# Hybrid attention trunk on one core: probability blocks turned four at a time, keys stored last 16 first, norms, splits and rotary rows in another order

## The chip, the core and the metric

The kernel is one program on one NeuronCore of a Trainium2 chip. The metric is the device time of one execution in microseconds (us), as a median of runs. TensorE is called PE, VectorE DVE, ScalarE ACT, GpSimd POOL; SP only issues DMAs.

## The reference

The reference runs four layers over T = 272 tokens (16 meta tokens, 256 of the sequence) with D = 1024. Each layer is a token mixer with 16 heads, then a gated MLP with a causal width-3 convolution; each half ends in `layer_norm(alpha*h + out)`. The mixers are, in order: FoX (forgetting attention), SWA (sliding window 128, two key/value heads, rotary, sinks), MLA (latent attention: nope part 64 wide, rotary part 32 wide, one rotary key shared by all heads), and FoX again.

```
s = q @ k.T * scale (+ decay[t] - decay[s])      # causal; SWA also within 128, meta keys always seen
p = softmax(s);  o = p @ v;  mix = o @ w_o
h = layer_norm(alpha*h + mix);  u = conv3(h @ w_in);  ffn = (silu(u_g) * u_v) @ w_out
h = layer_norm(alpha*h + ffn)
```

## The kernel before

Activations lie transposed: channels on partitions, all 272 tokens on the free axis. Every dense product is three fp32r matmuls of 128 x 128 weights by 272 columns (high weight by high input L385, high by low L388, low by high L389). A *unit* is 128 x 1024 fp32 weights (512 KB) in a ring of four slots: SP loads it (L344), ACT rounds it to `w_hi` (L839, `split_hi`), DVE subtracts to `w_lo` (L1260 inside `split_lo`). ACT and DVE each run a written order; a split for a unit three ahead stands at a fixed place in every turn of a loop, and DVE's split waits for ACT's of the same unit (`hi_ready`). All engines run their instructions strictly in that order and meet by semaphores.

Attention goes head by head, in pairs of heads, m = 0..7, overlapped with the projections of the next pair. The queries of a head stand in three chunks (`CHUNKS`: 16, 128, 128 queries, seeing 16, 144, 272 keys), side by side in 432 columns. For one head:

- PE: scores (L518 for FoX and SWA, L499 for MLA; FoX first adds the decay, L512), into a PSUM bank.
- DVE `mask_scores` (L1320): mask and row minimum. ACT `exps` (L886, L889): exponentials and row sums into `probs`. DVE `normalise` (L1335, L1338).
- PE `turn` (L535): six transposes of `probs`. ACT `copy_turned` (L901, L902): PSUM to `probs_t`.
- PE `mix` (L553): values by probabilities, three key blocks (272, 144 and 16 query columns) for two heads. ACT `out_hi` (L908) and DVE `out_lo` split the result for the output projection.

In SWA, DVE's turn m is: `out_lo(m-4)`, mask of heads 2m-4 and 2m-3, `rope_q(m-1)`, normalise of both heads, the split of a unit, and the evacuation of the query panel (L1565), for which PE's swap matmul (L690) waits. ACT's turn m is: `out_hi(m-4)`, exps of head 2m-4, two `copy_turned`, exps of head 2m-3, the `w_hi` of a unit. PE's: scores of pair m-2, turns of heads 2m-6 and 2m-5, swap, panel, mix of pair m-3; the last two turns stream the output projection (L404) in place of panels.

In MLA the reciprocal root of the key latent is made for all columns (ones matmuls L730, ACT root, DVE reciprocal L1640); the rotary key rows are copied to all 16 heads by POOL (L1217, L1222), the rotary query rows to `queries` by four 32-row DVE adds (`rope_r`); `take_k` (DVE, two ops) empties the key panel and stands between the two normalises; the next scores wait for it.

At the start of the MLP's second half (`output`, n odd) ACT loads its function table (L933) and then splits the first weights of `down`.

## Time and profile before

| | us |
|---|---|
| median of 3 runs (lowest, highest) | 1333.57 (1332.96, 1334.44) |
| profiled execution, its own time | 1333.88 |
| its span | 1332.1 |
| PE matmul busy | 1296.4 (97%) |
| DVE / ACT / POOL busy | 938.3 / 793.8 / 225.8 |

The span runs from the first instruction to the last; the execution's own time has 1.8 us more around it. PE is called busy from a matmul's start to its modelled end, which lies well after the next can start, so stalls are read from the distance of starts. The layers' attention stretches lie at about 47 to 130 us (FoX), 362 to 435 (SWA), 676 to 765 (MLA) and 1027 to 1110 (FoX).

### The profile page before, as it was taken

What the parts mean: (1) busy time and instruction counts of PE and PEld (TensorE: products, weight loads), DVE (VectorE), ACT (ScalarE), POOL (GpSimd) and SP (SyncE); (2) the same over time, 40 slices, a digit from 0 to 9 for tenths busy, and PEclk for the clock granted to TensorE, in tenths of its full rate; (3) what the DMA queues carried; (4) which work ended last, traced back from release to release, by engine and by line L of the source; (5) the groups of instructions that cost most, each with busy time, mean ns of one, the idle gap of its engine ahead of it and who ended that gap; (6) DMA issues with size and microseconds to landing.
All of it is one profiled execution on the core that took longest, in us unless ns stands there. A gap on an engine that the chain in (4) does not pass through costs nothing.

```text
span 1332.1 us, 29945 instructions
## 1 busy us (share of the span) xinstructions
PE 1296.4 (97%) x10381; PEld 1252.5 (94%) x10381; DVE 938.3 (70%) x1877; ACT 793.8 (60%) x1625; POOL 225.8 (17%) x208
## 2 busy tenths in 40 slices
PE   7999999999998999999998999999999999999997
PEld 7999999999887999999987899999999899999997
DVE  4765877765787877765678687776567667777665
ACT  4565666654565676664476667666446565766643
POOL 1000044420000034330001003433000000244300
PEclk9999999999999999999998999999999999999999
DMA  7432465556421455556442045555645334465562
GB/s 267 140 110 80 143 189 185 178 180 198 133 91 49 130 185 184 180 155 213 155 127 80 33 143 187 187 172 165 208 139 158 111 112 127 144 187 189 174 218 83
DMA packets 56723, 202.80 MB, mean 152 GB/s; under 512 B 6208, under 2 KB 8256, under 8 KB 56512
## 3 DMA queue, kind: packets, MB, share of 16 engines
q1 hardware_dynamic: 56640, 201.68, 47.4%
q8 instruction: 54, 0.88, 0.3%
q14 instruction: 29, 0.24, 0.1%
HBM read 200.61 MB, written 1.05 MB: 151 GB/s over the span
## 4 chain that ended last, share of the span: by engine, by line
PE 82%; DVE 7%; ACT 5%; issue 3%; DMA 1%; POOL 1%; ACTq 0%; DVEq 0%; POOLq 0%; SPq 0%
PE ps L385 23%; PE ps L389 22%; PE ps L388 22%; PE ps L535 2%; PE ps L553 2%; ACT probs L889 2%; DVE w_lo L1260 1%; PE ps L424 1%; PE ps L518 1%; PE ps L430 1%; PE ps L427 1%; ACT w_hi L839 1%; DMA raw<-in_weights 1%; POOL gated L1234 1%; DVE scores L1320 1%
## 5 line engine op out<-in xcount | busy, mean ns | idle before, releaser
L1260 DVE TENSOR_TENSOR w_lo<-raw,w_hi 128x1024 fp32r<-128x1024 f32 x377 | 461.1, 1225 | 230.3 <-ACT w_hi L839 228.9
L385 PE MATMUL ps<-h_hi,w_hi 128*128 128x272 f32 (+1 forms) x1752 | 508.6, 290 | 1.8 <-DVE q_rope L1526 1.0
L389 PE MATMUL ps<-h_hi,w_lo 128*128 128x272 f32 (+1 forms) x1752 | 505.8, 289 | 0.0
L388 PE MATMUL ps<-h_lo,w_hi 128*128 128x272 f32 (+1 forms) x1752 | 499.6, 285 | 0.0
L839 ACT ACTIVATE w_hi<-raw 128x1024 fp32r<-128x1024 f32 x377 | 395.0, 1050 | 147.7 <-PE ps L385 136.9
L385 PEld LDWEIGHTS ps<-h_hi,w_hi 128*128 128x128 f32 x1752 | 329.1, 188 | 8.4 <-issue 5.4
L388 PEld LDWEIGHTS ps<-h_lo,w_hi 128*128 128x128 f32 x1752 | 330.0, 188 | 0.3
L389 PEld LDWEIGHTS ps<-h_hi,w_lo 128*128 128x128 f32 x1752 | 328.9, 188 | 0.0
L385 PE MATMUL ps<-hid_hi,w_hi 128*128 128x272 f32 (+2 forms) x636 | 185.4, 292 | 2.2 <-DVE w_lo L1260 1.9
L388 PE MATMUL ps<-hid_lo,w_hi 128*128 128x272 f32 (+2 forms) x636 | 183.1, 288 | 0.0
L389 PE MATMUL ps<-hid_hi,w_lo 128*128 128x272 f32 (+2 forms) x636 | 183.0, 288 | 0.0
L1234 POOL TENSOR_TENSOR gated<-y 128x272 f32<-128x272 f32 x88 | 134.6, 1530 | 274.8 <-DVE y L1681 260.6
L1181 ACT ACTIVATE y<-ps,cst 128x272 f32<-128x272 f32 x176 | 100.0, 568 | 63.5 <-PE ps L389 61.8
L1208 POOL TENSOR_TENSOR h<-h,y 128x272 f32<-128x272 f32 x16 | 12.0, 774 | 707.1 <-ACT y L938 707.1
L385 PEld LDWEIGHTS ps<-hid_hi,w_hi 128*128 128x128 f32 x636 | 121.3, 191 | 3.7 <-issue 2.8
L388 PEld LDWEIGHTS ps<-hid_lo,w_hi 128*128 128x128 f32 x636 | 121.4, 191 | 0.4
L389 PEld LDWEIGHTS ps<-hid_hi,w_lo 128*128 128x128 f32 x636 | 121.2, 191 | 0.0
L1679 DVE SCALAR_TENSOR_TENSOR y<-ps,cst,y 128x271 f32<-128x271 f32 x176 | 87.4, 497 | 29.8 <-ACT y L1181 26.8
L1681 DVE SCALAR_TENSOR_TENSOR y<-ps,cst,y 128x270 f32<-128x270 f32 x176 | 87.8, 499 | 26.8 <-DVE y L1679 26.8
L889 ACT ACTIVATE probs<-scores,stats 16x16 f32<-16x16 f32 (+2 forms) x192 | 76.9, 401 | 46.0 <-DVE stats L1320 46.0
L388 PE MATMUL ps<-hid,w_hi 128*128 128x272 f32 (+1 forms) x288 | 82.1, 285 | 0.0
L389 PE MATMUL ps<-hid,w_lo 128*128 128x272 f32 (+1 forms) x288 | 82.0, 285 | 0.0
(184 smaller groups left out, 1727.3 us busy)
## 6 DMA issues: line engine op xcount, KB each, us to landing
raw<-in_weights SPq DMA_DIRECT2D x377, 512.0 KB, 3.7
cst<-in_consts SPq DMA_DIRECT2D x1, 1795.5 KB, 12.1
h<-in_x SPq DMA_DIRECT2D x2, 544.0 KB, 5.8
out<-h SPq DMA_DIRECT2D x8, 128.0 KB, 1.7
```

What stands on the lines that cost most here:

```text
L385: m = pe.matmul(b, whi, xhi, start=n == 0, stop=False)
L388: pe.matmul(b, whi, xlo, start=False, stop=False)
L389: m = pe.matmul(b, wlo, xhi, start=False, stop=n == len(tiles) - 1)
L535: return pe.transpose(b[0:keys_n, col:col + q], pr[0:q, c0:c0 + keys_n], ident[0:q, 0:q])
L553: ins = pe.matmul(ps[HD * s:HD * s + HD, 6, lo:T], v_tok[:, t, col:col + HD], probs_t[:, s, c0:c0 + T - lo], start=n == 0, stop=n == 2)
L839: act.activation(w_hi[slot][:], raw[slot][:], ACT.Copy).then_inc(hi_ready, 1)
L889: ins = act.activation(probs[0:r, hn % 4, PCOL[ch]:PCOL[ch] + hi], scores[0:r, s, SCOL[ch]:SCOL[ch + 1]], ACT.Exp, scale=-1.0, bias=stats[ ...
L1181: act.activation(y[:, j, :], bank(pu + j), ACT.Identity, scale=col(2), bias=col(3)).then_inc(conv_begun, 1)
L1234: pool.tensor_tensor(gated[:], y[:, 2 * slot, :], y[:, 2 * slot + 1, :], ALU.mult).then_inc(gate_mul, 1)
L1260: return dve.tensor_tensor(out_, a_, b_, op)
L1679: own.link(dve.scalar_tensor_tensor(yj[:, 1:T], b[:, 0:T - 1], col(1), yj[:, 1:T], ALU.mult, ALU.add))
L1681: dve.scalar_tensor_tensor(yj[:, 2:T], b[:, 0:T - 2], col(0), yj[:, 2:T], ALU.mult, ALU.add).then_inc(bank_free, 1)
```

## The change

Scores are laid out in another order: chunk 1 first (144 columns), chunk 0 (16), chunk 2 (272), and in chunk 2 and in `keys` the last 16 keys stand before the other 256. So the three narrow probability blocks (keys 128 to 143 of chunk 1, chunk 0, keys 256 to 271 of chunk 2) are 48 neighbouring columns, and `turn` is four transposes of 128 columns instead of six. `copy_turned` takes three instructions for two. The third matmul of `mix` has 48 columns, written in three groups of 16; its values (keys 128 to 143, 0 to 15, 256 to 271) are put under each other by two small DMAs issued by ACT (`corner_values`). Evacuations of keys become two instructions each (16 and 256 columns).

Beside this: in FoX `take_k` stands between the two splits; in SWA the first split follows the evacuation of keys and values, and DVE's turn has a new order; in MLA the key scale is spread by PE from the token-wise one (`lat_spread`), POOL's copies and DVE's 32-row adds become DMAs issued by ACT (one of 32 x 16 x 272 elements, and four of 32 x 272 for each of the four `place_rope`), and `take_k` stands straight after the masks; the table load of `down` comes one panel later.

```diff
-SCOL = (0, 16, 160, 432)
-SW = SCOL[3]
-
-PCOL = (0, P, 3 * P)
-PW = PCOL[2] + T
-
-
 TAIL = T - 2 * P
-PT1, PT2, PTW = T, T + P + TAIL, T + P + 2 * TAIL
+
+
+SCOL = ((P + TAIL, P + 2 * TAIL), (0, P + TAIL), (P + 2 * TAIL, P + 2 * TAIL + T))
+SW = SCOL[2][1]
+KCOL = ((TAIL, 2 * TAIL), (TAIL, P + 2 * TAIL), (0, T))
+
+
+TURNED = (0, P + 3 * TAIL, 2 * P + 3 * TAIL, P)
+PT1, PT2, PTW = T, T + P, T + P + 3 * TAIL
...
                 for ch, (lo, hi) in enumerate(CHUNKS):
-                    m = pe.matmul(ps[0:hi - lo, 2 + s, SCOL[ch]:SCOL[ch + 1]], q[:, lo:hi], key[:, 0:hi],
+                    m = pe.matmul(ps[0:hi - lo, 2 + s, slice(*SCOL[ch])], q[:, lo:hi], key[:, slice(*KCOL[ch])],
                                   start=True, stop=True)
                 m.then_inc(scored, 1)
...
-                def one(col, ch, key, keys_n=P):
-
-                    q = P
-                    c0 = PCOL[ch] + key
-                    return pe.transpose(b[0:keys_n, col:col + q], pr[0:q, c0:c0 + keys_n], ident[0:q, 0:q])
-
-
-                one(PT1 + TAIL - P, 1, P)
-                one(PTW - P, 2, 2 * P, TAIL)
-                one(0, 0, 0)
-                one(N_META, 1, 0)
-                one(N_META + P, 2, 0)
-                one(PT1 + TAIL, 2, P).then_inc(transposed, 1)
+                for n, col in enumerate(TURNED):
+                    t = pe.transpose(b[:, n * P:(n + 1) * P], pr[:, col:col + P], ident)
+                t.then_inc(transposed, 1)
 
             def mix(a, kind, m):
 
                 pe.wait_ge(pt_copied, HEADS * a + 2 * m + 2)
                 pe.wait_ge(o_split, PAIRS * a + m)
-                for n, (t, lo, c0) in enumerate(((0, 0, 0), (1, P, PT1), (2, 2 * P, PT2))):
+                if m == 0:
+                    pe.wait_ge(v_corners, 32 * (a + 1))
+                for t in range(3):
                     for s in range(2):
                         hn = 2 * m + s
                         col = (hn // 8 if kind == "swa" else hn) * HD
-                        ins = pe.matmul(ps[HD * s:HD * s + HD, 6, lo:T], v_tok[:, t, col:col + HD],
-                                        probs_t[:, s, c0:c0 + T - lo], start=n == 0, stop=n == 2)
+                        o, pt = ps[HD * s:HD * s + HD, 6], probs_t[:, s]
+                        if t < 2:
+                            dst, src = o[:, (0, N_META + P)[t]:T], pt[:, (0, PT1)[t]:(PT1, PT2)[t]]
+                        else:
+                            dst = o[:, 0:3 * P].rearrange("p (g c) -> p g c", g=3)[:, :, 0:TAIL]
+                            src = pt[:, PT2:PTW].rearrange("p (g c) -> p g c", g=3)
+                        ins = pe.matmul(dst, v_tok[:, t, col:col + HD], src, start=t == 0, stop=t == 2)
                 ins.then_inc(mixed, 1)
 
...
                         is_q = ks[0] == 0
                         for k in ks:
                             pe.wait_ge(lat_sq, k + 1)
-                            if not is_q:
-                                pe.matmul(ps[:, 6, 0:T], ones, y[:, k % 4, :], start=k == ks[0], stop=k == ks[-1])
...
                     swap(gated[:])
+                    pe.wait_ge(lat_scale, 1)
+                    for n, (lo, hi) in enumerate(((0, P), (P, 2 * P), (2 * P, T))):
+                        ins = pe.matmul(ps[:, 6, lo:hi], lat_col[0:hi - lo, 1, n:n + 1].broadcast_to([hi - lo, P]),
+                                        ident[0:hi - lo, 0:hi - lo], start=True, stop=True)
+                    ins.then_inc(lat_spread, 1)
                     for n in range(6):
...
+                            pe.wait_ge(rope_key, 16)
                         if m:
-                            pe.wait_ge(rope_key, (m - 1) // 2 + 1)
-                        if m:
-                            pe.wait_ge(roped, base + 2 + (m - 1) // 2)
+                            pe.wait_ge(rope_rows[(m - 1) // 2], 64)
                             pe.wait_ge(q_taken, m)
...
+            def corner_values(cols):
+
+                for n, chunk in enumerate((1, 0)):
+                    act.dma_start(v_tok[TAIL * n:TAIL * n + TAIL, 2, 0:cols],
+                                  v_tok[0:TAIL, chunk, 0:cols]).then_inc(v_corners, 16)
...
-                act.activation(probs_t[:, s, 0:PT2], ps[:, 4 + s, 0:PT2], ACT.Copy)
-                act.activation(probs_t[0:TAIL, s, PT2:PTW], ps[0:TAIL, 4 + s, PT2:PTW],
+                b = ps[:, 4 + s]
+                act.activation(probs_t[:, s, N_META:PT2], b[:, 0:3 * P], ACT.Copy)
+                act.activation(probs_t[0:32, s, PT2:PT2 + 2 * TAIL].rearrange("p (g c) -> p g c", g=2),
+                               b[0:32, 3 * P:4 * P].rearrange("p (g c) -> p g c", c=TAIL)[:, 0:8:7, :], ACT.Copy)
+                act.activation(probs_t[32:48, s, PT2 + 2 * TAIL:PTW], b[32:48, 4 * P - TAIL:4 * P],
                                ACT.Copy).then_inc(pt_copied, 1)
...
                     k = i * 4 + j
+                    if k == 1 and n % 2:
+                        act.preload_act_table_set(TABLES)
                     if k:
                         square(n, k - 1)
 
-                if n % 2:
-                    act.preload_act_table_set(TABLES)
...
                     latent_root(lat_col[:, 0, :], ps[:, 5, 0:3], 0).then_inc(lat_std, 1)
-                    latent_root(squares[:, 1, :], ps[:, 6, 0:T], 1).then_inc(lat_std, 1)
                     act.preload_act_table_set(TABLES)
...
+                    def place_rope(r):
+
+                        act.wait_ge(roped, ROPED0 + r + 1)
+                        for t in range(4):
+                            act.dma_start(queries[64:96, 4 * r + t, :],
+                                          totals[32 * t:32 * t + 32, r % 2, :]).then_inc(rope_rows[r], 16)
+
                     for r in range(2):
                         take_r(r)
+                    act.wait_ge(lat_spread, 1)
+                    act.activation(squares[:, 1, :], ps[:, 6, 0:T], ACT.Copy).then_inc(lat_std, 1)
                     split_unit(ur + AHEAD)
                     for n in range(6):
                         copy_vt(n)
                         if n == 0:
+                            act.wait_ge(key_roped, 1)
+                            act.dma_start(keys[64:96, :, :], rope_parts[:, 2 * T:3 * T].unsqueeze(1).broadcast_to(
+                                [32, HEADS, T])).then_inc(rope_key, 16)
                             split_unit(uv + AHEAD)
+                        if n == 2:
+                            place_rope(0)
                     split_unit(uv + 1 + AHEAD)
                     for r in range(2):
                         split_panel(a, "qk", r)
                         take_r(2 + r)
+                    place_rope(1)
+                    act.wait_ge(vt_copied, 6)
+                    corner_values(D)
                     for m in range(PAIRS + 1):
+                        if m in (3, 6):
+                            place_rope(m // 3 + 1)
                         if m >= 4:
...
-                    pool.wait_ge(key_roped, 1)
-                    pool.tensor_copy(keys[64:96, 0:4, :],
-                                     scores[0:32, 0, 0:T].unsqueeze(1).broadcast_to([32, 4, T])).then_inc(rope_key, 1)
-                    pool.wait_ge(rope_key, 1)
-                    pool.wait_ge(masked, HEADS * a + 2)
-                    for j in range(1, 4):
-                        pool.tensor_copy(keys[64:96, 4 * j:4 * j + 4, :],
-                                         keys[64:96, 0, :].unsqueeze(1).broadcast_to([32, 4, T])).then_inc(rope_key, 1)
-                    pool.wait_ge(rope_key, 4)
...
-                        copy(keys[:, m, :], b).then_inc(bank_free, 2)
+                        copy(keys[:, m, 0:TAIL], b[:, 2 * P:T])
+                        copy(keys[:, m, TAIL:T], b[:, 0:2 * P]).then_inc(bank_free, 2)
...
                         if m < PAIRS:
                             split_units(a, "qk", 0, 2 * m)
-                            if m == 0:
-                                take_k(m)
+                            take_k(m)
                             split_units(a, "qk", 0, 2 * m + 1)
-                            if m:
-                                take_k(m)
...
-                    split_units(a, "vk", 0, 0)
                     for j in range(2):
                         dve.wait_ge(panel_done, pv + j + 1)
                         vk_evac(0, j, bank(pv + j), pv + j)
+                    split_units(a, "vk", 0, 0)
...
-                                ins = copy(keys[64 * r:64 * r + 64, g, :], q_rope[64 * g:64 * g + 64, 0, :])
+                                src = q_rope[64 * g:64 * g + 64, 0, :]
+                                copy(keys[64 * r:64 * r + 64, g, 0:TAIL], src[:, 2 * P:T])
+                                ins = copy(keys[64 * r:64 * r + 64, g, TAIL:T], src[:, 0:2 * P])
...
-                    for m in range(PAIRS + 2):
-                        if m >= 4:
-                            out_lo(a, m - 4)
-                        if m >= 2:
+                    for m in range(PAIRS + 3):
+                        if m >= 3:
+                            normalise(a, kind, 2 * m - 5)
+                        if 2 <= m < PAIRS + 2:
                             mask_scores(a, kind, 2 * m - 4)
                             mask_scores(a, kind, 2 * m - 3)
                         if 1 <= m <= PAIRS:
                             rope_q(m - 1)
-                        if m >= 2:
-                            normalise(a, kind, 2 * m - 4)
-                            normalise(a, kind, 2 * m - 3)
+                        if 4 <= m < PAIRS + 2:
+                            out_lo(a, m - 4)
                         if m < PAIRS:
                             split_units(a, "q", 0, m)
+                        if 2 <= m < PAIRS + 2:
+                            normalise(a, kind, 2 * m - 4)
+                        if m < PAIRS:
                             dve.wait_ge(panel_done, pq + m + 1)
...
-                        for t in range(4):
-                            r = slice(32 * t, 32 * t + 32)
-                            ins = tt(queries[64:96, 4 * m + t, :], y[r, 0, :], y[r, 1, :], ALU.add)
-                        ins.then_inc(roped, 1)
+                        if m >= 2:
+                            dve.wait_ge(rope_rows[m - 2], 64)
...
-                        tt(keys[0:64, 2 * m, :], b[0:64], kv_rstd[0:64], ALU.mult)
-                        tt(keys[0:64, 2 * m + 1, :], b[64:128], kv_rstd[64:128], ALU.mult).then_inc(bank_free, 2)
+                        for s in range(2):
+                            r = slice(HD * s, HD * s + HD)
+                            tt(keys[0:64, 2 * m + s, 0:TAIL], b[r, 2 * P:T], kv_rstd[r, 2 * P:T], ALU.mult)
+                            ins = tt(keys[0:64, 2 * m + s, TAIL:T], b[r, 0:2 * P], kv_rstd[r, 0:2 * P], ALU.mult)
+                        ins.then_inc(bank_free, 2)
...
                     dve.wait_ge(lat_std, 2)
-                    own.link(dve.reciprocal(kv_rstd, kv_rstd))
...
+                        if m < PAIRS:
+                            take_k(m)
                         if 4 <= m < PAIRS:
                             out_lo(a, m - 4)
                         if m:
                             normalise(a, kind, 2 * m - 2)
-                        if m < PAIRS:
-                            take_k(m)
-                        if m:
                             normalise(a, kind, 2 * m - 1)
                         if m < PAIRS:
                             split_units(a, "qk", 0, 2 + 2 * m)
```

Two places show the new order. The first is DVE in a middle turn of SWA, between `rope_q` and the masks of the next turn. `hid_lo` is `out_lo`, `rinv` and `probs` are `normalise`, `w_lo` is the split, `queries<-ps` the evacuation. Before:

```order
L1335 RECIPROCAL rinv<-rinv 128x3 [waits dve_own]
L1338 TENSOR_SCALAR probs<-probs,rinv 16x16 [waits dve_own]
L1338 TENSOR_SCALAR probs<-probs,rinv 128x144
L1338 TENSOR_SCALAR probs<-probs,rinv 128x272
L1260 TENSOR_TENSOR rinv<-stats,sink_exp 128x3 [waits exped]
L1335 RECIPROCAL rinv<-rinv 128x3 [waits dve_own]
L1338 TENSOR_SCALAR probs<-probs,rinv 16x16 [waits dve_own]
L1338 TENSOR_SCALAR probs<-probs,rinv 128x144
L1338 TENSOR_SCALAR probs<-probs,rinv 128x272
L1260 TENSOR_TENSOR w_lo<-raw,w_hi 128x1024 [waits hi_ready]
L1565 TENSOR_SCALAR queries<-ps 128x272 [waits panel_done]
L1260 TENSOR_TENSOR hid_lo<-ps,hid_hi 128x272 [waits o_hi,bank_free]
```

And in the change:

```order
L1287 TENSOR_TENSOR queries<-y 128x272 [waits dve_own]
L1287 TENSOR_TENSOR hid_lo<-ps,hid_hi 128x272 [waits o_hi]
L1287 TENSOR_TENSOR w_lo<-raw,w_hi 128x1024 [waits hi_ready]
L1287 TENSOR_TENSOR rinv<-stats,sink_exp 128x3 [waits exped]
L1362 RECIPROCAL rinv<-rinv 128x3 [waits dve_own]
L1365 TENSOR_SCALAR probs<-probs,rinv 16x16 [waits dve_own]
L1365 TENSOR_SCALAR probs<-probs,rinv 128x144
L1365 TENSOR_SCALAR probs<-probs,rinv 128x272
L1596 TENSOR_SCALAR queries<-ps 128x272 [waits panel_done]
L1287 TENSOR_TENSOR rinv<-stats,sink_exp 128x3 [waits exped,bank_free]
L1362 RECIPROCAL rinv<-rinv 128x3 [waits dve_own]
L1365 TENSOR_SCALAR probs<-probs,rinv 16x16 [waits dve_own]
```

Both normalises stood ahead of the split; now both stand behind it, one on each side of the evacuation, and the masks of the next turn follow the second.

The second is ACT in MLA at the start of turn m = 6 (`place_rope(3)`), in the change:

```order
L914 ACTIVATE probs_t<-ps 16x16
L1134 DMA queries<-totals 32x272 [waits roped]
L1134 DMA queries<-totals 32x272 x3
L920 ACTIVATE hid_hi<-ps 128x272 [waits mixed]
L898 ACTIVATE probs,stats<-scores,stats 16x16 [waits transposed,masked]
```

Four DMAs now stand in ACT's queue ahead of `out_hi` and of the exponentials.

## Rows read from the trace of the kernel before

**Rows 1.** The page: the chain that ended last, by engine
```profile
PE 82%; DVE 7%; ACT 5%; issue 3%; DMA 1%; POOL 1%; ACTq 0%; DVEq 0%; POOLq 0%; SPq 0%
```

**Rows 2.** Groups of PE by shape: columns as on the page; transposes, ones matmuls
```profile
L535 PE MATMUL ps<-cst,probs 128*128 128x128 f32 x320 | 47.8, 274 | 0.0
...
L730 PE MATMUL ps<-y,cst 128*128 128x272 f32 x4 | 1.1, 392 | 0.0
```

**Rows 3.** Timeline of PE in FoX: start, us, instruction [idle before, releaser]
```profile
56.02 0.47 PE L512 MATMUL ps<-dec,pick 64*128 64x432 f32 x2 [0.99 <-issue]
...
60.47 1.47 PE L535 MATMUL ps<-cst,probs 128*128 128x128 f32 x12
```

**Rows 4.** Timeline of DVE in FoX, the second key evacuation
```profile
55.48 0.43 DVE L1499 COPY keys<-ps 128x272 f32<-128x272 f32 x1
```

**Rows 5.** Timeline of DVE in SWA, one turn
```profile
401.85 0.21 DVE L1320 CUSTOM_DVE_ANT_0 scores<-ps,cst,neg_sinks 16x16 f32<-16x16 f32 x1
...
406.63 0.17 DVE L1260 TENSOR_TENSOR rinv<-stats,sink_exp 128x3 f32<-128x3 f32 x1 [0.80 <-ACT probs L889]
...
407.66 1.20 DVE L1260 TENSOR_TENSOR w_lo<-raw,w_hi 128x1024 fp32r<-128x1024 f32 x1
408.80 0.42 DVE L1565 TENSOR_SCALAR queries<-ps 128x272 f32<-128x272 f32 x1
409.25 0.44 DVE L1260 TENSOR_TENSOR hid_lo<-ps,hid_hi 128x272 fp32r<-128x272 f32 x1
409.61 0.21 DVE L1320 CUSTOM_DVE_ANT_0 scores<-ps,cst,neg_sinks 16x16 f32<-16x16 f32 x1
```

**Rows 6.** Timeline of ACT in SWA, the same turn
```profile
402.81 0.30 ACT L886 ACTIVATE sink_exp<-stats,cst 128x3 f32<-128x3 f32 x1 [2.75 <-DVE stats L1320]
...
404.21 0.49 ACT L901 ACTIVATE probs_t<-ps 128x416 f32<-128x416 f32 x1
...
405.13 0.28 ACT L886 ACTIVATE sink_exp<-stats,cst 128x3 f32<-128x3 f32 x1
...
406.51 1.04 ACT L839 ACTIVATE w_hi<-raw 128x1024 fp32r<-128x1024 f32 x1
```

**Rows 7.** Timeline of PE at the start and the end of SWA
```profile
362.83 0.40 PE L385 MATMUL ps<-h_hi,w_hi 128*128 128x272 f32 x1 [0.99 <-DVE q_rope L1526]
...
427.38 1.00 PE L553 MATMUL ps<-probs_t,v_tok 128*64 128x272 f32 x12 [1.28 <-ACT probs_t L902]
```

**Rows 8.** Windows: length, busy by engine, PEclk (granted clock), DMA; SWA, then MLA
```profile
400.00:420.00 20.00, 18.71 (x154) 15.92 (x152) 17.91 (x74) 11.74 (x49) 0.00 (x0) 1.00 0.26 80
716.00:720.00 4.00, 4.00 (x19) 3.37 (x18) 3.42 (x16) 2.70 (x11) 0.00 (x0) 0.60 0.33 75
```

**Rows 9.** Timeline of PE in MLA
```profile
715.41 2.74 PE L499 MATMUL ps<-keys,queries 96*16 96x16 f32 x12 [2.27 <-DVE keys L1260]
```

**Rows 10.** Timeline of DVE in MLA, work that the change removes or shortens
```profile
693.05 1.84 DVE L1640 RECIPROCAL h<-h 128x272 f32<-128x272 f32 x1
...
704.78 1.98 DVE L1338 TENSOR_SCALAR probs<-probs,rinv 16x16 f32<-16x16 f32 x3
...
709.33 1.78 DVE L1260 TENSOR_TENSOR queries<-y 32x272 f32<-32x272 f32 x4
```

**Rows 11.** Timeline of DVE in MLA, one turn
```profile
738.59 0.22 DVE L1320 CUSTOM_DVE_ANT_0 scores<-ps,cst,q_scale 16x16 f32<-16x16 f32 x1
...
743.72 1.23 DVE L1260 TENSOR_TENSOR w_lo<-raw,w_hi 128x1024 fp32r<-128x1024 f32 x1
...
744.98 0.22 DVE L1320 CUSTOM_DVE_ANT_0 scores<-ps,cst,q_scale 16x16 f32<-16x16 f32 x1
```

**Rows 12.** Timeline of SP, one weight load issued
```profile
385.74 0.33 SPq L344 DMA_DIRECT2D raw<-in_weights  x1
```

**Rows 13.** Timeline of ACT and of PE at the start of the last `down`
```profile
1261.82 1.28 ACT L933 ACT_TABLE_LOAD   x1
...
1265.58 0.35 PE L385 MATMUL ps<-hid_hi,w_hi 128*128 128x256 f32 x1 [1.91 <-DVE w_lo L1260]
```

56 lines of the change are left out of this document (35 added, 21 removed).

## Prediction

> **What bounds the kernel now.** I read the page first: PE is busy 97% of the span (the table above), and 82% of the chain that ended last lies on it [rows 1]. Where PE never waits, a matmul taken away is time gained. Busy time cannot tell where that is, so I next went through the distances between PE's starts in the timeline of each attention stretch, then through DVE and ACT beside every long one. The stretches differ. In FoX PE streams without a pause in each turn of the loop. In SWA PE waits in every turn, and a loop through DVE and ACT sets the pace. In MLA PE waits mostly for DVE. The MLP halves are PE's, but for one stall.
>
> The sum is made against the profiled execution's 1333.9 us; the median of the runs is 0.3 us less. Within 0.2%, 2.7 us, a measurement of this kernel cannot tell a change from none.
>
> **The transposes, and FoX.** Twelve transposes of a pair take 1.47 us, the last of them 0.27 by itself [rows 2, 3], so they follow each other every (1.47 - 0.27)/11 = 0.109 us. Four fewer a pair are 0.44 us, and 32 pairs would give 14.0 us if PE bound all of them. It does in FoX: 16 pairs, 7.0 us. The rest of FoX is cheap. `mix` has 16 columns fewer in one matmul and 32 more in the other; at the transposes' 0.109 us for 128 columns, two passes each, that is +0.03 us a pair, at most 0.9 us in all and perhaps nothing, since matmuls of 16 columns are not shorter in proportion. I take 0. The longer `copy_turned` and the two ACT DMAs fall where ACT waits for masks. DVE's key copy in two parts costs some 0.1 us more; the `mix` ahead of the scores hides it. In the first pair no `mix` does: PE started the second scores at 56.02 and DVE had begun the key copy they wait for only at 55.48 [rows 3, 4], after two splits. With the copy between the splits it starts when its panel is done, 55.1, and PE at 55.75: 0.27 us gained, twice. FoX: **-7.5 us**.
>
> **SWA.** DVE's masks start at 401.85 and again at 409.61: 7.76 us a turn [rows 5]. I follow the turn by starts. Mask to exps of the even head 0.96; these exps 1.40; two turned copies 0.92; exps of the odd head 1.38; `w_hi` and hand-over 1.15, up to DVE's `w_lo` at 407.66; `w_lo` 1.14; panel evacuation 0.45; `out_lo` 0.36 [rows 5, 6]. These sum to 7.76, so this loop is the bound and PE's transposes are not. In the change `w_lo` still waits for the `w_hi` that ACT makes after the odd head's exps, while both normalises, which now stand in the shadow of that wait, come behind it: even head, evacuation, odd head, and only then the masks. One normalise is 407.66 - 406.63 = 1.02 us [rows 5]. `out_lo` leaves the loop (-0.36), two normalises enter (+2.05), and the third copy instruction adds some 0.1: 9.55 us a turn, +1.79. Five turns (m = 3 to 7) run this loop: +8.9. Turn 2 has no copies and no `out_lo`: +1.9. At the start, PE waits for a copy that stands behind a split and resumes at 362.83 [rows 7]; the copy comes first now, 0.8 us sooner, of which eight instead of four key copies take back 0.4: -0.4. At the end, `mix` waits 1.28 us for the turned copies [rows 7], which come 0.1 us later after the scores, so the transposes saved ahead of it only lengthen the wait: 0. SWA would gain 0.4 and lose 10.8: **+10.4 us**, instead of the 3.5 us that its transposes are worth. The work that I cost at nothing, PE's, is hidden by the loop with 9.55 - 6.2 = 3.3 us of idleness a turn, 6.2 being PE's own work, added up from the distances of its starts without the waits.
>
> That idleness has a second price. In MLA PE stood for 2.5 us (starts) at 715.41, and in the four microseconds after it the granted clock was 0.60: most of it at 1.2 GHz, not 2.4 [rows 8, 9]. In SWA, with waits under a microsecond in each turn, it was 1.00 [rows 8]. In the change PE would wait some 2.3 us at a stretch, and 1.1 more after the even head's transposes. I expect turns with half the clock; a panel of 24 matmuls, 0.1 us longer each (272 columns at 1.2 instead of 2.4 GHz), is 2.4 us longer, less than the 3.3 idle, so the loop stays the bound until the last turns, where output weights stream and nothing covers: up to 1.5 us, I take **+0.7**. The Trainium skill (TensorE: Matmul & The Clock Gate, Part 1: The HAM clock gate) says that the clock halves after PE has been idle and is given back after sustained work. By it the clock would go up and down in every turn, which is a case of its own below.
>
> **MLA.** Removed: the ones matmuls, four of 0.27 us or less [rows 2]; DVE's 1.84 us reciprocal and, four times, 1.78 us of 32-row adds, for which one add of 0.44 stands [rows 10]; POOL's copies, beside which a normalise took 1.98 us where it takes 0.69 elsewhere [rows 10]. Added: three small PE matmuls (some 0.5 us), 0.2 us a `take_k`, and DMA issues in ACT's queue. For one issue the trace has only SP's, 0.33 us [rows 12]; ACT may pay from nothing to 0.6. I take 0.4, near SP's, 1.6 us for a `place_rope`. The turn, from mask to mask, is 738.59 to 744.98, and `w_lo` at 743.72, waiting for ACT, ends just before the second [rows 11]: again the loop through ACT. Moving `take_k` frees PE, but not this loop, which stays near 6.3 us where a unit is split. By turns of masks (1 to 7) I get 7.0, 6.3, 6.7, 6.35, 6.3, 7.1, 5.9 us, where now 8.9, 6.5, 6.8, 7.75, 6.4, 6.4, 6.0 stand. The gain is in turn 1 (POOL, adds) and turn 4 (adds); turn 6 pays for four DMA issues. The first mask comes 0.8 us later, since ACT's ten DMA issues ahead delay a unit. Masks then end 3.1 - 0.8 = 2.3 us sooner; the last scores, which waited for `take_k` behind a normalise, some 3.4 us sooner than now, at some 751 us; two pairs of transposes after them are PE's again, 0.9. MLA: **-4.2 us** (-1.5 to -6, by issues of 0.6 or of nothing and by whether PE falls to half clock once).
>
> **The last `down`.** ACT loads its table for 1.28 us, then splits; PE waits 1.91 us until 1265.58 [rows 13] and streams about 15 matmuls at half clock afterwards. The load behind six splits leaves a wait of 0.7, and the clock likely stays. **-2.8 us** (-1.3 if it doesn't). In the other layers PE has no such stall.
>
> **Sum**: -7.5 + 10.4 + 0.7 - 4.2 - 2.8 = -3.4: 1330.5 for the execution, **1330.2 us** for the median.
>
> **The rivals.**
> 1. *Transposes pay everywhere.* If the SWA loop is not what I read, because DVE finds its units split and only its own 6.9 us of work a turn count, SWA gains 4 to 5 us and the time is about 1316. For it: DVE no longer waits 0.80 us for the odd head's exps [rows 5], and ACT has more idle time than DVE. Against it: the split's wait, in both listings. Chance 0.12.
> 2. *MLA returns little.* ACT's DMA issues cost 0.6 us or hold it longer, and its loop gets slower where now it is even: MLA -1, the clock at the end of SWA +1.5: 1334, no difference. Chance 0.18.
> 3. *Half clock reaches the loop: slower.* At 1.2 GHz PE's whole turn in SWA (8 transposes, swap, panel, `mix`, scores, 6.2 us) would be 12 us, over the 9.55 of the loop. It decides from the point where over half of a turn is at half clock; with three quarters of it a turn is 10.8, +1.2 on seven turns, 8 us: 1338. The rows of MLA speak for it, the full clock after each burst against it. With milder forms, chance 0.12.
>
> **How the numbers follow.** My forecast has 0.58, with its own range from 1327 to 1333.5 (MLA 2.5, clock 1.5, `mix` 0.9). About two thirds of it lie under 1330.9, the bound of 0.2%: with rival 1, faster 0.52. The rest with rival 2 gives same 0.36, and rival 3 slower 0.12. The range leaves out rival 1 and the far part of 3: 1325 to 1336.
>
> **What would show it.** FoX turns of 9.36 us instead of 9.80 (from transposes to transposes). SWA: masks 9.5 us apart with DVE idle some 2.5 us ahead of `w_lo`; PE 3 us idle a turn; granted clock under 1 there. Masks under 7.3 us apart would refute the largest term. MLA: no 1.98 us normalise; four DMA issues of about 0.4 us on ACT in turns 3 and 6; scores over by 3.4 us less. The last `down`: a stall of 0.7 us, and no half clock behind it. If FoX's turns shrink by less than 0.4 us, the third matmul of `mix` is dearer than I took it.

## The result, and the profile after

The change makes the kernel slower: 1341.32 us (median of 4 runs, 1340.45 to 1342.22) against 1333.26 (4 runs, 1331.83 to 1334.44), a ratio of 1.0061 (95% interval 1.0044 to 1.0078). I had forecast 1330.2 in a range from 1325 to 1336. The profiled execution has a span of 1339.4 us, where before's had 1332.1.

The same instruction can be looked up in both traces, so the sum can be read stage by stage. The first column is where ACT starts the named `w_hi` split (the last row: where PE starts its last matmul).

| up to here | before | after | behind by | this stage | forecast |
|---|---|---|---|---|---|
| split 104: FoX and its MLP | 361.68 | 357.78 | -3.89 | -3.9 | -3.75 |
| split 120: SWA | 448.67 | 459.72 | +11.05 | **+14.9** | +11.1 |
| split 192: MLP | 675.33 | 685.82 | +10.49 | -0.6 | 0 |
| split 208: MLA | 771.10 | 784.23 | +13.13 | **+2.6** | -4.2 |
| split 284: MLP | 1009.16 | 1022.71 | +13.55 | +0.4 | 0 |
| split 308: FoX | 1114.25 | 1124.12 | +9.88 | -3.7 | -3.75 |
| last matmul: MLP with the last `down` | 1322.75 | 1330.08 | +7.34 | -2.5 | -2.8 |

FoX and the last `down` came out as forecast. SWA, forecast as the one loss, lost a third more. MLA has the wrong sign. Against the forecast, SWA is 3.8 us behind and MLA 6.8: together that is the whole miss.

The page, to stand beside the table of before:
```profile
PE 1287.1 (96%) x10255; PEld 1242.0 (93%) x10255; DVE 929.9 (69%) x1903; ACT 813.9 (61%) x1689; POOL 219.0 (16%) x204
...
PE 38%; DVE 4%; ACT 2%; issue 2%; POOL 1%; ACTq 1%; DVEq 0%; POOLq 0%
```
PE is busy 9.3 us less and the kernel is longer all the same; what was saved on PE has become waiting. (The chain's shares add up to less than half of the span, so the chain is not complete here and I don't read it.)

**FoX**, PE, the transposes of the first two pairs (before: [rows 3]):
```profile
59.97 1.04 PE L535 MATMUL ps<-cst,probs 128*128 128x128 f32 x8
...
69.44 0.82 PE L535 MATMUL ps<-cst,probs 128*128 128x128 f32 x6
```
Eight transposes for twelve (a row counts only what falls into its window, here six of the second pair's eight). The transposes of later pairs start 9.36 or 9.37 us apart, forecast 9.36; before it was 9.80. The first distance here is 9.47.

**SWA**, DVE, one turn (before: [rows 5]):
```profile
386.32 0.22 DVE L1347 CUSTOM_DVE_ANT_0 scores<-ps,cst,neg_sinks 16x16 f32<-16x16 f32 x1
...
392.68 1.23 DVE L1287 TENSOR_TENSOR w_lo<-raw,w_hi 128x1024 fp32r<-128x1024 f32 x1 [3.03 <-ACT w_hi L842]
393.82 0.15 DVE L1287 TENSOR_TENSOR rinv<-stats,sink_exp 128x3 f32<-128x3 f32 x1
...
395.30 0.16 DVE L1287 TENSOR_TENSOR rinv<-stats,sink_exp 128x3 f32<-128x3 f32 x1
...
396.32 0.22 DVE L1347 CUSTOM_DVE_ANT_0 scores<-ps,cst,neg_sinks 16x16 f32<-16x16 f32 x1
```
From mask to mask it is 10.00 us, where before had 7.76 and I forecast 9.55. The picture is the forecast one: DVE waits 3.03 us for `w_hi`, and then both normalises follow `w_lo`, ahead of the next masks. ACT in the same turn (before: [rows 6]):
```profile
387.29 0.30 ACT L895 ACTIVATE sink_exp<-stats,cst 128x3 f32<-128x3 f32 x1 [3.40 <-DVE stats L1347]
...
388.68 0.46 ACT L911 ACTIVATE probs_t<-ps 128x384 f32<-128x384 f32 x1
389.05 0.17 ACT L912 ACTIVATE probs_t<-ps 32x32 f32<-32x32 f32 x1
389.24 0.17 ACT L914 ACTIVATE probs_t<-ps 16x16 f32<-16x16 f32 x1
389.43 0.49 ACT L911 ACTIVATE probs_t<-ps 128x384 f32<-128x384 f32 x1
...
390.20 0.30 ACT L895 ACTIVATE sink_exp<-stats,cst 128x3 f32<-128x3 f32 x1
...
391.60 1.04 ACT L842 ACTIVATE w_hi<-raw 128x1024 fp32r<-128x1024 f32 x1
```
By starts: mask to exps 0.97, exps 1.39, two copies **1.52** (before 0.92), exps 1.40, `w_hi` 1.08, `w_lo` 1.14, normalise 1.02, evacuation 0.45, normalise 1.03: 10.00. The missing 0.45 lies in the copies, for which I had allowed 0.1 a pair and which cost 0.6.

PE waits for the normalise ahead of every pair of transposes, 2.3 us at 375.05, 404.97 and 424.97 and 0.74 to 0.78 at the three others. The clock, in windows of one turn (length, busy by engine, granted clock, DMA):
```profile
385.00:395.00 10.00, 8.44 (x59) 7.17 (x59) 6.76 (x29) 5.68 (x22) 0.00 (x0) 0.83 0.18 55
395.00:405.00 10.00, 6.85 (x59) 5.73 (x59) 6.76 (x29) 5.68 (x22) 0.00 (x0) 1.00 0.16 52
```
Of the five windows three read 0.83 and two 1.00. So PE did fall to 1.2 GHz for a third of such a turn. The Trainium skill (TensorE: Matmul & The Clock Gate, Part 1: The HAM clock gate) has the clock halve after idleness and come back after sustained work; the trace agrees in kind. The turns with and without half clock are equally long, 10.00 us, so the half clock was covered, as forecast. PE's waits show where it went: the three short ones stand at the end of the three slowed turns, the 2.3 us ones behind turns at full clock.

It was not covered behind the last masks. There `mix` waits longer than before (1.28 us, [rows 7]), and the clock falls. PE's row and its window in the change, then the same two places in e3_early_split, where the same wait left the clock alone:
```profile
437.29 0.45 PE L554 MATMUL ps<-probs_t,v_tok 128*64 128x272 f32 x2 [2.19 <-ACT probs_t L914]
...
437.00:441.00 4.00, 3.71 (x23) 3.46 (x24) 1.38 (x6) 2.11 (x10) 0.00 (x0) 0.61 0.00 0
```
```profile
424.76 0.94 PE L554 MATMUL ps<-probs_t,v_tok 128*64 128x272 f32 x10 [2.19 <-ACT probs_t L914]
...
424.80:428.80 4.00, 3.73 (x34) 3.26 (x35) 1.38 (x6) 3.23 (x14) 0.00 (x0) 1.00 0.00 0
```

**MLA**, PE at the first scores before and in the change, then ACT ahead of them and in turn 6, then the window behind them ([rows 9] and the second window of [rows 8] show a like wait of before, at its third scores):
```profile
701.01 0.52 PE L499 MATMUL ps<-keys,queries 96*16 96x16 f32 x3 [1.07 <-DVE keys L1260]
```
```profile
714.05 2.47 PE L502 MATMUL ps<-keys,queries 96*16 96x16 f32 x9 [2.75 <-ACT queries L1127]
```
```profile
709.24 2.44 ACTq L1134 DMA_DIRECT2D queries<-totals  x4
711.72 1.24 ACTq L884 DMA_DIRECT2D v_tok<-v_tok  x2
713.00 0.80 ACT L1127 ACTIVATE queries<-ps 64x272 f32<-64x272 f32 x2 [3.39 <-issue]
...
752.29 0.40 ACT L920 ACTIVATE hid_hi<-ps 128x272 fp32r<-128x272 f32 x1 [1.03 <-issue]
```
```profile
717.00:721.00 4.00, 4.00 (x18) 3.87 (x17) 0.94 (x6) 2.54 (x11) 0.00 (x0) 0.50 0.37 131
```
And later, PE at `mix`:
```profile
741.81 1.00 PE L554 MATMUL ps<-probs_t,v_tok 128*64 128x272 f32 x12 [1.36 <-DVE hid_lo L1287]
```
One issue takes ACT 2.44 / 4 = 0.61 us, and six of them stand directly ahead of the queries that the first scores wait for. PE is idle 2.75 us, then at 1.2 GHz for the whole window behind it. The wait of `mix` is another one, for `out_lo`; it stands in four turns, 1.36 us in the first and 0.81 in the others. The normalise of 1.98 us beside POOL's copies is gone; none of the change's takes over 0.35 us an instruction.

**The last `down`** (before: [rows 13]):
```profile
1274.02 0.36 PE L388 MATMUL ps<-hid_hi,w_hi 128*128 128x256 f32 x1 [0.50 <-DVE w_lo L1287]
```
The wait is 0.50 us instead of 1.91, forecast 0.7, with the full clock behind it.

### The profile page after: what moved, and what is told of

Its sections match the earlier page's. It is cut to its first block and busy times, and to the rows that moved or that the text cites. A ratio compares the mean times of both kernels' runs of the same rounds, so it can differ in the third digit from the quotient of the medians.

```text
span 1339.4 us, 29778 instructions
## 1 busy us (share of the span) xinstructions
PE 1287.1 (96%) x10255; PEld 1242.0 (93%) x10255; DVE 929.9 (69%) x1903; ACT 813.9 (61%) x1689; POOL 219.0 (16%) x204
## 5 line engine op out<-in xcount | busy, mean ns | idle before, releaser
L388 PE MATMUL ps<-h_hi,w_hi 128*128 128x272 f32 (+1 forms) x1752 | 510.7, 292 | 1.4 <-DVE w_lo L1287 0.6
L388 PEld LDWEIGHTS ps<-h_hi,w_hi 128*128 128x128 f32 x1752 | 330.7, 189 | 8.4 <-issue 5.4
L388 PE MATMUL ps<-hid_hi,w_hi 128*128 128x272 f32 (+2 forms) x636 | 184.5, 290 | 1.0 <-DVE w_lo L1287 0.5
L388 PEld LDWEIGHTS ps<-hid_hi,w_hi 128*128 128x128 f32 x636 | 120.1, 189 | 2.4 <-issue 1.4
```

The costliest lines, as they stand in the source:

```text
L388: m = pe.matmul(b, whi, xhi, start=n == 0, stop=False)
```

## The experiments

Theory A is the prediction's own: in each stage a loop of instructions from mask to mask sets the turn, and it can be added up by starts. Rivals B to K stand in the expectations. The kernel before was timed again beside each group of runs, with medians of 1332.59 (e1 to e4), 1332.21 (e5b to e8b) and 1332.57 (e9c to e11c) where the result has 1333.26, so a difference between runs of two groups is uncertain by about 1 us. Stages are read from one profiled execution of each kernel.

**e1_swa_old_order.** The change, with DVE's SWA turn as it was before:
```diff
-                    for m in range(PAIRS + 3):
-                        if m >= 3:
-                            normalise(a, kind, 2 * m - 5)
-                        if 2 <= m < PAIRS + 2:
+                    for m in range(PAIRS + 2):
+                        if m >= 4:
+                            out_lo(a, m - 4)
+                        if m >= 2:
                             mask_scores(a, kind, 2 * m - 4)
                             mask_scores(a, kind, 2 * m - 3)
                         if 1 <= m <= PAIRS:
                             rope_q(m - 1)
-                        if 4 <= m < PAIRS + 2:
-                            out_lo(a, m - 4)
+                        if m >= 2:
+                            normalise(a, kind, 2 * m - 4)
+                            normalise(a, kind, 2 * m - 3)
                         if m < PAIRS:
                             split_units(a, "q", 0, m)
-                        if 2 <= m < PAIRS + 2:
-                            normalise(a, kind, 2 * m - 4)
...
```


> The changed kernel with the SWA turn of DVE in the order of before: both normalises ahead of the split, out_lo at the turn's head. Theory A (the loop mask, exps, copies, exps, w_hi, w_lo, evacuation sets the turn, and the two normalises behind w_lo are what lengthened it): masks 8.3 us apart instead of 10.0 (the 7.76 of before and 0.6 for a pair's third copy instructions), so 5 x 1.7 + 1.9 for turn 2 and about 1 us at the end are returned: 1330 us. Theory B (the new layout with its copies and evacuations is what costs, the order of DVE's turn is harmless): turns stay near 10.0 and the time within 2 us of 1341.

Measured: 1331.80 us (10 runs), 0.9994 of before (0.9985 to 1.0004), 9.5 us faster than the change (8.9 with each taken against its own before). Masks are 8.39 us apart:
```profile
391.51 0.21 DVE L1347 CUSTOM_DVE_ANT_0 scores<-ps,cst,neg_sinks 16x16 f32<-16x16 f32 x1
...
399.90 0.21 DVE L1347 CUSTOM_DVE_ANT_0 scores<-ps,cst,neg_sinks 16x16 f32<-16x16 f32 x1
```
The order of one engine's turn decides between slower and no difference. Theory B falls as the main cause; what it holds of the layout is the rest, SWA's 4.8 us over before in e1's splits.

**e2_new_order_alone.** The same edit the other way round, on the kernel before.

> The kernel before with nothing changed but the order of DVE's SWA turn, which is that of the change. Theory A: masks 7.76 - 0.36 + 2.05 = 9.45 us apart, turn 2 longer by 1.9, about 1 us more at the end where PE streams at half clock: 8.5 + 1.9 + 1 = 11.4 us slower, 1344.7. Theory B: 1333, masks 7.8 us apart.

Measured: 1343.65 us, 1.0088 of before (1.0071 to 1.0104), 11.1 us slower. The wait for `w_hi` is there without any new layout, and masks are 9.39 us apart:
```profile
389.30 0.22 DVE L1320 CUSTOM_DVE_ANT_0 scores<-ps,cst,neg_sinks 16x16 f32<-16x16 f32 x1
...
395.04 1.22 DVE L1260 TENSOR_TENSOR w_lo<-raw,w_hi 128x1024 fp32r<-128x1024 f32 x1 [2.42 <-ACT w_hi L839]
...
398.69 0.22 DVE L1320 CUSTOM_DVE_ANT_0 scores<-ps,cst,neg_sinks 16x16 f32<-16x16 f32 x1
```

**e3_early_split.** The change, with the split first in ACT's SWA turn:
```diff
+                        if m < PAIRS:
+                            split_panel(a, "q", m)
                         if m >= 2:
                             exps(a, kind, 2 * m - 4)
...
                             exps(a, kind, 2 * m - 3)
-                        if m < PAIRS:
-                            split_panel(a, "q", m)
```


> The changed kernel, but ACT makes a SWA turn's w_hi ahead of the exps of the even head, where it waits 3.4 us for the masks, and not behind those of the odd head. Theory A: w_lo no longer waits, the loop through ACT is cut, and the turn is DVE's own work, 6.9 to 7.1 us by the distances of its starts; 5 x 2.9 + 2 to 3 us for turn 2 and the end: 1323 to 1326. Theory C (order and splits matter little because the odd head's normalise waits for exps and copies in the same chain anyway: mask 0.97, exps 1.39, copies 1.52, exps 1.40, normalise 1.03, which alone are 6.3 us and with PE's scores behind them 8 or more): 8 to 9.5 us a turn, 1331 to 1338.

Measured: 1329.96 us (10 runs), 0.9980 of before (0.9971 to 0.9990). Turns are 7.95 us: much shorter, but not 7.0; theory A named the wrong chain here, and C's numbers (8 to 9.5 us a turn, 1331 to 1338 in all) are missed narrowly, with a reason that is not the one found:
```profile
391.41 1.06 ACT L842 ACTIVATE w_hi<-raw 128x1024 fp32r<-128x1024 f32 x1 [2.18 <-PE ps L388]
```
`w_hi` takes the slot of a unit that PE has used up when its next panel begins (L388), and PE begins it only after both heads' transposes. The split had got into a new loop: normalise, transposes, panel, `w_hi`, exps, copies, exps. By starts, from the odd head's normalise at 388.92 to the next: to the panel 1.90, to `w_hi` 0.59, to the exps 0.97, to the copies 1.38, to the other exps 1.52, to the normalise 1.59, which is 7.95.

**e4_pool_issues.** The change, with the rotary DMAs of MLA issued by POOL:
```diff
-                            act.wait_ge(key_roped, 1)
-                            act.dma_start(keys[64:96, :, :], rope_parts[:, 2 * T:3 * T].unsqueeze(1).broadcast_to(
-                                [32, HEADS, T])).then_inc(rope_key, 16)
...
-                        if n == 2:
-                            place_rope(0)
...
-                    place_rope(1)
...
-                        if m in (3, 6):
-                            place_rope(m // 3 + 1)
...
+                    pool.wait_ge(key_roped, 1)
+                    pool.dma_start(keys[64:96, :, :], rope_parts[:, 2 * T:3 * T].unsqueeze(1).broadcast_to(
+                        [32, HEADS, T])).then_inc(rope_key, 16)
+                    place_rope(0)
+                    place_rope(1)
+                    place_rope(2)
+                    place_rope(3)
```


> The changed kernel with MLA's 17 DMAs of rotary rows issued by POOL, which is idle there, in place of ACT; the two for the corner values stay on ACT. Theory A (ACT is held 0.62 us by each issue, and MLA's shortfall is mostly that): the first scores, now at 714.06, start 2 us earlier, the 1.0 us waits at the heads of turns 3 and 6 go, one stretch at half clock may go: 3 to 5 us faster than the change, 1337. Theory D (MLA's loss lies in the wait for the rows to land and in take_k's four instructions, not in ACT's issues; POOL's issues take longer): within 1 us of 1341, or slower.

Measured: 1337.49 us, 1.0043 of before (1.0026 to 1.0060), 3.8 us faster than the change (3.2 against its own before): theory A, not D.
```profile
706.68 1.96 POOL L1246 DMA_DIRECT2D queries<-totals  x4 [4.04 <-DVE totals L1292]
```
```profile
711.42 1.25 PE L502 MATMUL ps<-keys,queries 96*16 96x16 f32 x8 [1.21 <-DVE keys L1292]
```
POOL pays 0.49 us an issue, and no wait in this trace is put down to it. PE's wait fell from 2.75 to 1.21 us, for DVE now, and the window behind it reads a granted clock of 1.00. By the same splits as in the table, MLA now stands 2.9 us better than before, not 2.6 worse. (The profiled execution is the fastest of the four, 1335.63 us.) Of the 5.6 us between them, 3.1 are the first mask, which comes that much sooner after the split of the MLP's end (number 192), and 2.2 are turn 1, 6.89 us for 9.05.

**e5b_three_copies.** The kernel before, 416 columns copied as 384 and 32.

> The kernel before, in which each copy_turned takes three instructions for two: the 416 columns are copied as 384 and 32 (the same bytes, nothing else changed). The changed kernel's pair of copies took 1.52 us of ACT's loop in SWA where before's took 0.92, and I had allowed 0.1. Theory A (the instruction itself costs ACT some 0.2 to 0.3 us a head, whatever it copies): SWA turns of 8.1 to 8.35 us instead of 7.76, six turns, 2 to 3.5 us slower in all. Theory E (the cost is not the third instruction but the strided or displaced rows of the changed copies): turns of 7.76 to 7.9, within 1 us of before.

Measured: 1334.39 us (10 runs), 1.0014 (1.0005 to 1.0024). Turns are 7.87 us, theory E, though the whole is 2.2 us slower where E had within 1:
```profile
397.04 0.17 ACT L902 ACTIVATE probs_t<-ps 128x32 f32<-128x32 f32 x1
397.12 0.16 ACT L903 ACTIVATE probs_t<-ps 16x16 f32<-16x16 f32 x1
397.19 0.46 ACT L901 ACTIVATE probs_t<-ps 128x384 f32<-128x384 f32 x1
```
A third instruction as such costs 0.05 us a head, just what I had allowed. The change's copies, of 32 and 16 rows, take 0.18 and 0.20 from start to start.

**e9c_copy_shapes** and **e12_copy_rows** ask why. Both are the kernel before with narrow columns copied by rows 0 to 31, 32 to 63 and 64 to 127, in e9c as two groups of 16 columns far apart, in e12 as 32 neighbouring ones.

> The kernel before with the same 416 columns of copy_turned copied in five pieces: 128 rows x 272 and x 112 columns, then two groups of 16 columns 128 apart, for rows 0 to 31, 32 to 63 and 64 to 127 each; the last 16 x 16 stays. In e5b a plain 32-column copy over all 128 rows took 0.077 us from its start to the next and the 16 x 16 behind it 0.063; in the change the two narrow copies take 0.18 and 0.20. Theory H (a copy with two groups of columns is dearer): all three strided copies take about 0.18, and the contiguous 16 x 16 behind them 0.06. Theory I (rows that begin at 32 or later, or a change of rows, are dearer): the strided copy of rows 0 to 31 takes 0.07 to 0.1, those of rows 32 and 64 about 0.18. Theory J (few rows are dearer): 32-row copies 0.18, the 64-row one less. ACT's loop is longer by the sum, so SWA's turns are some 0.5 to 1.2 us longer.

> e9c_copy_shapes with contiguous columns: the kernel before with the 416 columns of copy_turned copied as 128 rows x 384 and then 32 contiguous columns for rows 0 to 31, 32 to 63 and 64 to 127 each; the 16 x 16 stays. In e9c all three copies with two groups of columns took 0.18 to 0.20 us from start to start, the 16 x 16 behind them 0.05 to 0.08. Theory H (the groups are what is dear): the three contiguous copies take 0.06 to 0.08 each. Theory I (a copy of another set of rows than the one ahead of it, or rows that begin at 32 or 64, is dear, as the contiguous 16 x 16 at row 32 of the changed kernel with its 0.20 suggests): the copy of rows 0 to 31 takes under 0.1, those at 32 and 64 about 0.2.

Measured: 1356.70 us (2 runs) and 1351.53 (one run). SWA's turns are 9.03 and 8.92 us, about 1.2 longer, and FoX's are longer too (10.8 and 10.7), which I had not said. e9c, then e12:
```profile
395.83 0.57 ACT L906 ACTIVATE probs_t<-ps 32x32 f32<-32x32 f32 x3
396.41 0.17 ACT L907 ACTIVATE probs_t<-ps 16x16 f32<-16x16 f32 x1
396.49 0.37 ACT L901 ACTIVATE probs_t<-ps 128x272 f32<-128x272 f32 x1
```
```profile
395.55 0.57 ACT L903 ACTIVATE probs_t<-ps 32x32 f32<-32x32 f32 x3
396.14 0.17 ACT L904 ACTIVATE probs_t<-ps 16x16 f32<-16x16 f32 x1
396.22 0.46 ACT L901 ACTIVATE probs_t<-ps 128x384 f32<-128x384 f32 x1
```
Both give 0.18, 0.20 and 0.20 us for the three copies, and 0.08 for the 16 x 16 behind them. So the groups cost nothing (H falls), few rows are not dear (J falls), and I fails as I put it: the copy of rows 0 to 31 is dear too. What fits all is the instruction that comes next. Where it begins at the same row, it starts 0.06 to 0.08 us later, while the first still runs; where it begins at another row, it starts 0.18 to 0.20 later, when the first (0.17 to 0.19 long) is over. The change's copies cross rows twice a head, 0 to 32 and back. The trace of before had the case already, in MLA, where ACT's two copies of queries read rows from 0 and rows from 64:
```profile
699.22 0.80 ACT L1110 ACTIVATE queries<-ps 64x272 f32<-64x272 f32 x2 [1.00 <-PE ps L389]
```
Each is 0.39 us long, and the second starts 0.41 after the first, while the `w_hi` behind it starts 0.30 after the second.

**e6b_pool_out_lo_first.** e4, with MLA's `out_lo` ahead of `take_k` on DVE.

> The kernel of e4_pool_issues with one more edit: in MLA's DVE turn out_lo stands ahead of take_k and not behind it. In the change mix waits 0.97 us in each of turns 4 to 7 for out_lo, which stands behind take_k, which waits for the key panel. Theory A (this wait, made by the moved take_k, is what keeps MLA's turns at 6.65 where 6.3 was forecast): those turns shrink to 6.2 to 6.3, the bound of DVE's own work; 1.2 to 2 us faster than e4. Theory F (the turns are bound by DVE's or ACT's work anyway): turns stay at 6.65, no difference.

Measured: 1335.42 us (10 runs), 1.0022 (1.0012 to 1.0031), 2.1 us faster than e4 (1.7 against its own before; the runs of the two overlap). Transposes are 6.23 to 6.39 us apart from the third pair on, where e4 has 7.20, 6.65, 6.65: theory A. From the first mask on, MLA is 1.8 us shorter than in e4, as forecast. By the splits the whole stage gains only 0.3 us, since ahead of the first mask, in code that is the same, this execution ran at a granted clock of 0.57 (688.00:692.00) and lost 1.5 us.

**e7b_late_lo** and **e8b_mid_split**, both on top of e6b:
```diff
                         if 1 <= m <= PAIRS:
+                            split_units(a, "q", 0, m - 1)
                             rope_q(m - 1)
                         if 4 <= m < PAIRS + 2:
                             out_lo(a, m - 4)
-                        if m < PAIRS:
-                            split_units(a, "q", 0, m)
```
and, on ACT instead,
```diff
                             exps(a, kind, 2 * m - 4)
+                        if m < PAIRS:
+                            split_panel(a, "q", m)
                         if m >= 3:
                             copy_turned(a, 2 * m - 6)
...
-                        if m < PAIRS:
-                            split_panel(a, "q", m)
```


> e6b with one more edit, in SWA: DVE makes w_lo one turn later, behind the next turn's masks, from the w_hi that ACT made at the end of its turn; ACT's order stays that of the change. e3 stopped at 7.95 us a turn because w_hi then waited for PE's panel to begin, and exps for w_hi. Theory A (the chain is whatever stands between mask and mask): it is now mask, exps, copies, exps, normalise, 0.97 + 1.39 + 1.52 + 1.40 + 1.03 = 6.3 us, below DVE's own 6.9 to 7.0, so turns of 7.0: 5 x 3.0 + 2 us less than e6b, near 1319. Theory G (PE's order scores, turns, panel, mix with its waits sets at least 7.7 whatever DVE does): 7.7 to 8, near 1323.

> e6b with one more edit, in SWA: ACT makes w_hi between the exps of the even head and the copies; DVE's order is that of the change. Theory A: the chain is mask, exps, w_hi, copies, exps, normalise, 0.97 + 1.39 + 1.06 + 1.52 + 1.40 + 1.03 = 7.35 us a turn, unless w_hi is late for DVE's w_lo: 5 x 2.65 + 2 us less than e6b, near 1321, some 2 us above e7b. Theory G: 7.7 to 8, as e7b.

Measured: **1317.63 us**, 0.9890 of before (0.9874 to 0.9907), and 1320.08, 0.9909 (0.9893 to 0.9926). Turns are 6.89 us in e7b and 7.46 in e8b. e7b:
```profile
388.90 0.22 DVE L1352 CUSTOM_DVE_ANT_0 scores<-ps,cst,neg_sinks 16x16 f32<-16x16 f32 x1
...
390.64 1.21 DVE L1292 TENSOR_TENSOR w_lo<-raw,w_hi 128x1024 fp32r<-128x1024 f32 x1
...
395.80 0.22 DVE L1352 CUSTOM_DVE_ANT_0 scores<-ps,cst,neg_sinks 16x16 f32<-16x16 f32 x1
```
```profile
381.70:409.40 27.70, 26.61 (x235) 23.41 (x233) 26.86 (x114) 23.96 (x92) 0.00 (x0) 1.00 0.25 77
```
`w_lo` waits for nothing; DVE is busy 26.86 of 27.70 us and is the bound by its work. Theory G falls. One split, a turn later, is worth 17.8 us (e7b against e6b), 15.3 of them in SWA by the splits.

**e10c_load_later_alone.** The kernel before, with only the table load moved.

> The kernel before with nothing changed but the table load of down, which comes one panel later. Theory A: the last down's stall falls from 1.91 us to 0.7 or less, the clock stays at 2.4 GHz behind it, and the end comes 2.7 us sooner: ratio 0.998. Theory K (the gain seen at that place comes from another timing that the whole change made, or reappears as a stall for the late split): less than 1 us.

Measured: 1330.91 us (10 runs), 0.9987 (0.9978 to 0.9997). Windows around the start of the last `down`, before and then here:
```profile
1266.00:1270.00 4.00, 4.00 (x24) 4.00 (x22) 3.18 (x4) 1.08 (x2) 0.00 (x0) 0.57 0.77 240
```
```profile
1266.00:1270.00 4.00, 4.00 (x37) 4.00 (x36) 2.27 (x2) 1.11 (x2) 0.00 (x0) 1.00 0.87 284
```
The wait and the half clock are gone. By PE's starts that is 3.7 us: from the last matmul of `up` to the end it takes 63.41 us instead of 67.10. But ACT's splits, 0.72 us ahead of before's at number 352, are 2.87 ahead at the end: 2.15 gained, and the medians differ by 1.7. The two don't contradict each other. In before's profile PE had come 1.5 us sooner out of the `up`, with ACT and POOL no sooner, and stood waiting for them; that lead was worth nothing. So theory A is right in kind and 0.5 to 1 us too high. The profile of before also shows the dear case: e5b and e12 keep the load where it was, and there PE waits 0.39 and 0.40 us at this place, with the full clock behind it. From split 352 to 360 before takes 22.75 us, e5b 21.41, e10c 20.59.

**e11c_corners_later.** e7b, with the corner DMAs behind the splits of turn 0.

> e7b with ACT's two remaining DMA issues in MLA (the corner values) behind the splits of turn 0 and no longer ahead of it. mix needs them only in turn 3. Theory A (whatever ACT does ahead of take_q delays the first scores): they start up to 1.2 us sooner, their stall of 1.25 us shrinks to under 0.4, and turn 1 has no stretch at half clock: 1 to 2.5 us faster than e7b, 1316. Theory D (the first scores wait for take_k and the panel as well): 0 to 0.5 us.

Measured: 1318.58 us, 0.9896 (0.9879 to 0.9913), no better than e7b. PE's first wait is 1.21 us, as it was, for `take_k`: theory D. (ACT issued the two at 693.59 and 694.16, where e7b has 692.30, so they moved less than their place in the program.) The granted clock behind it reads 0.57 here and 1.00 in e7b, after the same wait, and turn 1 takes 8.28 us for 6.89.

## Why the prediction was wrong

- **FoX, forecast -7.5 us: right.** -3.9 and -3.7, turns of 9.36 us.
- **SWA, forecast +10.4 and +0.7: the mechanism of the turns is right, a size is off, and the small term for the clock fails.** e1 and e2 show it from both sides: undoing the order gives back 9.5 us, the order alone costs 11.1. Of the 3.8 us missing, 5 x 0.45 = 2.3 are the sentence "the third copy instruction adds some 0.1". It was right for a plain instruction (e5b) and wrong for one that begins at another row (e12): 0.6. Another 0.5 is the last turn between masks, 7.04 for 6.55, for which I had no term; it has these copies too. The rest lies behind the last masks, 1.6 us for the 0.7 that I had put there, and that term was wrong in kind. I had priced half clock from the new order's idleness; with the order alone (e2) this stretch is as long as before, 24.73 us from the last masks to split 120. What costs is the layout: `mix` waits 2.19 us instead of 1.28 for the copies that I had 0.1 later, which makes the stretch 0.4 us longer (25.13 in e3, e4, e6b and e8b), and where the clock falls after that wait, as in the change, e1, e7b and e11c, it is 1.5 to 1.6 longer.
- **MLA, forecast -4.2: wrong by 6.8 us, and this made the wrong sign.** Two steps failed. The first is "I take 0.4, near SP's": an issue takes ACT 0.61 us, just over the upper end of my range. But the price was the smaller part. I let ten issues delay the first mask by 0.8 us, through a unit's split. In fact there are eleven, and the last six, four and two, stand right ahead of ACT's copy of the queries, so the first mask came 716.03 - 10.49 - 702.25 = 3.3 us later, and the half clock after that wait made turn 1 9.05 us instead of 7.0. (How much of it falls into the turn is chance: e1 has the same MLA program and the same wait of 2.75 us, and its turn 1 takes 7.55.) The second step is "frees PE, but not this loop": the moved `take_k` put `out_lo` behind a wait for the key panel, and `mix` behind `out_lo`, as the row at 741.81 shows. I had listed who waits for `take_k`, and not who is queued behind it. By masks, the 6.8 us are 2.5 for the first mask, 2.05 for turn 1, 1.4 for turn 7 (7.33 for 5.9; 6.50 in e6b) and 0.9 for the rest. With both mended MLA stands 4.7 us better than before in e7b, and 3.2 in e6b with its half clock ahead of the stage, so the terms on the saved work were sound in sum.
- **The last `down`, forecast -2.8: right**, -2.6 by ACT's splits in the change (9.86 behind at number 352, 7.24 at 360), and 1.7 to 2.15 alone. I had added the wait and the half clock as PE shows them, and not asked whether PE's time ahead of a wait is worth its full length, nor whether the half clock comes there in every execution.
- **The rivals.** Rival 2 had the mechanism of MLA (issues of 0.6 us, a loop held up) and stopped at -1 where it was +2.6. Rival 3 needed half clock over half of a SWA turn; it got a third, and the turn didn't grow. The slower outcome came by rival 2's way in MLA and by a larger SWA loop, not by rival 3's.
- **The chances.** The two large terms were of opposite signs and nearly equal. A sum of -3.4 us between terms of 11 and 15 deserved more than 0.12 for slower: the bounds of MLA alone, had they held a first mask 3 us later, would have passed zero.

## What to carry over

In a kernel whose engines run written orders, time a turn as a loop: go from one instruction to its next occurrence through whatever releases each step, and ask of every moved instruction whether it leaves that loop or enters it. What waits longest (here a split that waits for another engine) belongs last, or a turn later. An instruction that only issues DMAs occupies its queue like any other; put it on an engine that nobody waits for.

## What was not expected of the hardware

- ACT overlapped two copies that follow each other only where both begin at the same row: short ones are 0.06 to 0.08 us from start to start against 0.18 to 0.20. It is enough that the rows read differ (the copies of queries above) or the rows written: in the change a 16-row copy into `v_tok` from row 32 is 0.68 us long and the next instruction starts 0.71 after it (706.13 to 706.84), where before, with the same copy at row 0, it is 0.59. The Trainium skill (ScalarE: Activation LUTs, What ACT_TABLE_LOAD costs) says that back-to-back ACTIVATEs overlap by about 93 ns. The plain case agrees (0.170 long, 0.077 to the next, 0.093 of overlap); where the row changes, no overlap is left in any of these copies.
- A DMA issue occupies ACT 0.61 us, POOL 0.49, SP 0.33 [rows 12] for these transfers. It can begin while the ACTIVATE ahead of it still runs: in e4 ACT's first issue starts at 708.12, beside a copy that runs from 707.63 to 708.49.
- The same wait of 1.21 us left the clock at 2.4 GHz in e4, e6b, e7b and e8b and was followed by 1.2 GHz in e11c; a wait of 2.2 us did so in four of eight kernels at the end of SWA (the change, e1, e7b and e11c against e3, e4, e6b and e8b). Such a stretch made the same work 1.1 to 1.5 us longer where nothing covered it. What decides between them is not settled by these runs, so a stage read from one trace can be off by that much.
